# Two roots cut in two slots, the cheap scores ahead of a subtraction, and rows brought to all partitions by DMA instead of by TensorE

## The reference

```
# branch A: gated DeltaNet, 8 heads, prompt in chunks
q, k = l2_normalize(silu(conv(q))) * 128**-0.5, l2_normalize(silu(conv(k)))
beta = sigmoid(b);  g = -exp(a_log) * softplus(a + dt_bias)
G = cumsum(g)                              # per head and chunk
decay = where(i >= j, exp(G_i - G_j), 0)
L = where(i > j, (k*beta) @ k.T * decay, 0)
sol = triangular_solve(I + L, [v*beta, k*beta*exp(G)])
s, o = scan over the chunks with exp(G), decay, sol
y_a = rms_norm(o) * gdn_norm * silu(z)
# branch B: latent attention over the pages of a cache
for page in page_table:
    kn = rms_norm(c @ w_uk);  v = c @ w_uv
    s = (qn . kn + qr . kr) * scale;  partial softmax, merged at the end
# x + (g_a * (y_a @ w_ya) + g_b * (y_b @ w_yb)) @ w_o, then x + relu(..)**2 @ w_down
```

## Time and profile before

| | us |
|---|---|
| median of 3 runs | 1426.72 |
| lowest, highest run | 1419.31, 1428.12 |
| the profiled execution, own time | 1426.71 |
| its span in the profile | 1424.9 |
| what lies around the span | 1.8 |

### The profile page before, as it was taken

How to read it: one execution, slowest core, us unless ns; L and a number is a source line. 1 busy time by engine, 2 the same in 40 slices (tenths; PEclk the granted TensorE clock), 3 DMA queues, 4 the chain that set the end, 5 groups by cost and what they waited for, 6 DMA issues and landing times.

```text
span 1424.9 us, 30022 instructions
## 1 busy us (share of the span) xinstructions
PE 1385.5 (97%) x9428; PEld 1170.5 (82%) x9428; DVE 1013.0 (71%) x3674; ACT 859.0 (60%) x2780; POOL 296.0 (21%) x339
## 2 busy tenths in 40 slices
PE   8999999999999999999999999899999999999998
PEld 7877887877777777878778787678778999999998
DVE  5867667787877787777878777768666667777543
ACT  5536678686666866666865667566784453444332
POOL 3012222223332222322222312222241000000000
PEclk9999999999999999999999999999999999999999
DMA  9442326643457443365443463334644565555551
GB/s 284 119 118 57 92 53 146 161 104 73 95 116 162 105 98 76 87 154 125 93 108 85 107 141 83 74 80 104 178 89 157 167 237 177 178 178 177 177 180 59
DMA packets 282890, 180.05 MB, mean 126 GB/s; under 512 B 183072, under 2 KB 229696, under 8 KB 282728
## 3 DMA queue, kind: packets, MB, share of 16 engines
q1 hardware_dynamic: 282418, 177.86, 48.9%
q10 hardware_dynamic: 318, 0.33, 0.1%
HBM read 134.32 MB, written 6.77 MB: 99 GB/s over the span
## 4 chain that ended last, share of the span: by engine, by line
PE 78%; DVE 9%; ACT 8%; issue 3%; SPq 2%; DMA 1%; POOL 0%; DVEq 0%; ACTq 0%
PE ps L2058 13%; PE ps L2060 12%; PE ps L2059 12%; PE ps L2462 6%; PE ps L2463 6%; PE ps L2464 6%; ACT ksq L894 2%; PE ps L2133 2%; DVE prod L1284 2%; PE ps L2410 2%; PE ps L2411 2%; PE ps L2080 2%; PE ps L2134 2%; ACT cTr L881 2%; PE ps L2135 2%
## 5 line engine op out<-in xcount | busy, mean ns | idle before, releaser
L2058 PE MATMUL ps<-ukh,cTh 128*128 128x512 f32 x1024 | 418.7, 409 | 21.4 <-DVE sparts L1284 21.1
L894 ACT ACTIVATE ksq<-ps 128x128 f32<-128x128 f32 x1024 | 268.2, 277 | 243.3 <-PE ps L2060 242.9
L2060 PE MATMUL ps<-ukh,cTl 128*128 128x512 f32 x1024 | 402.2, 393 | 0.0
L2059 PE MATMUL ps<-ukl,cTh 128*128 128x512 f32 x1024 | 402.2, 393 | 0.0
L2058 PEld LDWEIGHTS ps<-ukh,cTh 128*128 128x128 f32 x1024 | 194.3, 190 | 77.7 <-issue 37.4
L1284 DVE CUSTOM_DVE_ANT_0 prod<-ps,qb 128x128 f32<-128x128 f32 x1024 | 234.9, 286 | 6.1 <-ACT ksq L894 5.1
L2060 PEld LDWEIGHTS ps<-ukh,cTl 128*128 128x128 f32 x1024 | 193.8, 189 | 43.0
L2059 PEld LDWEIGHTS ps<-ukl,cTh 128*128 128x128 f32 x1024 | 194.3, 190 | 34.2
L746 POOL TENSOR_TENSOR rk<-kss,mhalf 128x8 f32<-128x8 f32 x128 | 219.5, 1715 | 10.7
L894 ACT ACTIVATION_READ_ACCUMULATOR ksq<-ps 128x1 f32 x1024 | 212.9, 208 | 0.0
L881 ACT ACTIVATE cTr<-turned 128x1024 uint16<-128x1024 uint16 x126 | 174.6, 1386 | 3.6 <-DMA turned<-planes 3.6
(11 more groups left out here) (504 smaller groups left out, 2700.8 us busy)
## 6 DMA issues: line engine op xcount, KB each, us to landing
clat<-cache_mla SPq DMA_DIRECT2D x128, 256.0 KB, 2.6
wraw<-w_in SPq DMA_DIRECT2D x16, 1024.0 KB, 5.2
wraw<-w_up SPq DMA_DIRECT2D x16, 1024.0 KB, 5.4
wraw<-w_down SPq DMA_DIRECT2D x16, 1024.0 KB, 5.0
braw<-w_in SPq DMA_DIRECT2D x24, 512.0 KB, 4.1
crope<-cache_mla SPq DMA_DIRECT2D x128, 32.0 KB, 2.4
qb<-scratch SPq DMA_DIRECT2D x16, 256.0 KB, 3.7
sst<-state_gdn SPq DMA_DIRECT2D x32, 128.0 KB, 3.5
```

The lines of the kernel that those rows point to most:

```text
L894: i = nc.scalar.activation(ksq[m % 3], ps[:, k % 3, P * h:P * h + P], ACT.Square, accum_out=kss[:, n // 4 % 2, n % 4, h0 + h:h0 + h + 1]). ...
L2058: mm(out, cTh[:, n % 2, c], ukh[:, c, cols], start=c == 0, stop=False)
L2059: mm(out, cTh[:, n % 2, c], ukl[:, c, cols], start=False, stop=False)
L2060: i = mm(out, cTl[:, n % 2, c], ukh[:, c, cols], start=False, stop=c == 3)
```

## The change

- VectorE, page loop: `scored` of the group before now stands ahead of `split_lo(n + 1)`, with the same waits.
- `newton` is cut in two. `newton_start` does the reciprocal, at steps 16 and 44. The rest stands in the slot behind step 16, which was empty (`ROOT`), and at step 45. Steps 17 and 46, where TensorE takes the results, stay where they were.
- The four `spread_row` of a pair for decay sums and beta are gone, with VectorE's copies out of PSUM for the decay sums (L1515) and the split of `rw`. In their place, SP writes the 2 x 8 rows of `rw` to a tensor in HBM once (slot 34), waits until both writes have landed, and reads for each pair the two rows of decay sums into `eg` and a row of beta each into `br0` and `br1`, with a broadcast to all 128 partitions. This reading is at slot 34 for pair 0 and at step 44 of the pair before for the others. `br1` lies in SBUF where `rwh` lay, `br0` where `rwl` lay. VectorE reads beta from SBUF now.

```
-STEPS = list(range(14)) + [None, 14, 15, 16, None] + list(range(17, 47))
+ROOT = 47
+STEPS = list(range(14)) + [None, 14, 15, 16, ROOT] + list(range(17, 47))
...
+            def decay_rows_in(b):
+                if b >= 1:
+                    sp.wait_ge(S("a_read"), a_count(f"out3_{b - 1}"))
+                    sp.wait_ge(S("beta_read"), 2 * b)
+                sp.dma_start(eg[:], decay_rows[H + 2 * b:H + 2 * b + 2, :].rearrange("(o h) t -> o h t", o=1).to_broadcast([P, 2, T])).then_inc(S("eg_landed"), 16)
+                for hh in range(2):
+                    sp.dma_start(beta[hh][:], decay_rows[2 * b + hh:2 * b + hh + 1, :].to_broadcast([P, T])).then_inc(S("beta_landed"), 16)
...
                 if k == 44 and b + 1 < HP:
                     pair_rows_in(b + 1)
+                    decay_rows_in(b + 1)
...
                 if i == B_START - 1:
                     pair_weights(2)
+                    sp.wait_ge(S("g_ready"), 1)
+                    sp.wait_ge(S("decay_act"), 4)
+                    for r in range(2):
+                        sp.dma_start(decay_rows[H * r:H * r + H, :], rw[32 * r:32 * r + H, :]).then_inc(S("decay_rows_landed"), 16)
+                    sp.wait_ge(S("a_read"), a_count("bg"))
+                    sp.wait_ge(S("decay_rows_landed"), 32)
+                    decay_rows_in(0)
...
+            def newton_start(rows_, count):
+                v.wait_ge(S("row_sqrt"), count)
+                y = lr[0:rows_, 1]
+                V.reciprocal(y, y).then_inc(S("row_inverse"), 1)
+
             def newton(rows_, count, scale, sem):
-                v.wait_ge(S("row_sqrt"), count)
+                v.wait_ge(S("row_inverse"), count)
                 x, y, t_ = lr[0:rows_, 0], lr[0:rows_, 1], lt3[0:rows_]
-                link(V.reciprocal(y, y))
...
                 if k in (12, 13):
                     hh = k - 12
-                    V.tensor_copy(eg[:, hh, :], bank(f"gr{hh}")[:, 0:T]).then_inc(S("a_read"), 1)
-                    v.wait_ge(S("a_read"), a_count(f"gr{hh}_{b}"))
+                    v.wait_ge(S("eg_landed"), 16 * (b + 1))
...
                 if k == 16:
+                    newton_start(P, 2 * b + 1)
+                if k == ROOT:
                     newton(P, 2 * b + 1, consts[:, C_RSQ], "row_rstd")
                 if k in (15, 16):
...
-                    p_ = bank(f"br{hh}")
+                    v.wait_ge(S("beta_landed"), 32 * (b + 1))
+                    p_ = beta[hh]
...
                 if k == 44:
+                    newton_start(64, 2 * b + 2)
+                if k == 45:
                     newton(64, 2 * b + 2, 1.0, "row_rstd")
...
                 beside(2 * n)
-                if n + 1 < NT:
-                    split_lo(n + 1)
                 if n == 1:
                     scored(0, 0)
                 if n:
                     scored(n - 1, 1)
+                if n + 1 < NT:
+                    split_lo(n + 1)
...
-                if k in (12, 13):
-                    pe.wait_ge(S("rw_split"), 1)
-                    spread_row(f"gr{k - 12}_{b}", P, 32 + 2 * b + k - 12, rwh[:], rwl[:])
...
-                if k in (15, 16):
-                    spread_row(f"br{k - 15}_{b}", P, 2 * b + k - 15, rwh[:], rwl[:])
```

More of the change, by code:

```diff
@@ L136 @@
 F_END = F_ATT + H + 3
-STEPS = list(range(14)) + [None, 14, 15, 16, None] + list(range(17, 47))
+ROOT = 47
+STEPS = list(range(14)) + [None, 14, 15, 16, ROOT] + list(range(17, 47))
 B_START, B_SLOTS = F_END + 6, len(STEPS)
-PAIR_A = ([f"p{j}" for j in range(6)] + ["gr0", "gr1", "l2r", "br0", "br1", "lb0", "lb1", "lb2", "lb3", "qk", "kk", "qks", "kqs", "kqsT", "x1", "t1"])
+PAIR_A = ([f"p{j}" for j in range(6)] + ["l2r", "lb0", "lb1", "lb2", "lb3", "qk", "kk", "qks", "kqs", "kqsT", "x1", "t1"])
 for _s in range(2, LEVELS):
@@ L301, in build @@
         assert e <= C_NEG.stop * 4
-        rwh, e = place("rwh", [P, T], F32R, C_NEG.start * 4)
+        br1, e = place("br1", [P, T], F32, C_NEG.start * 4)
         assert e <= C_NEG.stop * 4
@@ L352, in build @@
         bwl, o = place("bwl", [P, KC, P], F32R, o)
-        rwl, _ = place("rwl", [P, T], F32R, o)
+        br0, _ = place("br0", [P, T], F32, o)
         rw, o = place("rw", [P, T], F32, o)
@@ L417, in build @@
         ps = ctx.enter_context(nc.psum_tensor("ps", [P, 8, 512], F32))
+        beta = [br0, br1]
+        decay_rows = nc.dram_tensor("decay_rows", (2 * H, T), F32, kind="Internal").ap()
         scratch = nc.dram_tensor("scratch", (NS, D), F32, kind="Internal").ap()
@@ L1440, in decay_steps @@
                     V.tensor_copy(bg[:].rearrange("p n c -> p (n c)"), a_bank("bg")[:, 0:128]).then_inc(S("a_read"), 1)
-                    v.wait_ge(S("decay_act"), 4)
-                    split(rw[:], rwh[:], rwl[:], "rw_split")
             def conv(b, j):
@@ L1530, in pair_dve @@
                     v.wait_ge(S("decay_exp"), 3 * b + 1)
-                    p_ = bank(f"br{hh}")
+                    v.wait_ge(S("beta_landed"), 32 * (b + 1))
+                    p_ = beta[hh]
                     us = slice(2 * hh, 2 * hh + 2)
                     V.tensor_tensor(lT[:, us, :].rearrange("p u n -> p (u n)"), dt_[:, us, :].rearrange("p u n -> p (u n)"), p_[:, 0:TP], ALU.mult)
-                    V.tensor_copy(small(7)[:, :, hh], p_[:, TP:T]).then_inc(S("a_read"), 1)
+                    V.tensor_copy(small(7)[:, :, hh], p_[:, TP:T]).then_inc(S("beta_read"), 1)
                 if k == 17:
-                    v.wait_ge(S("a_read"), a_count(f"br1_{b}"))
+                    v.wait_ge(S("beta_read"), 2 * b + 2)
                     link(V.tensor_tensor(lT[:], lT[:], level_mask(C_STRICT), ALU.mult))
```

## The result

The changed kernel takes 1436.03 us (median of 10 runs, 1432.01 to 1438.68), the kernel before 1426.52 us beside it (1419.31 to 1429.33). The ratio is 1.0069 with a 95% interval of 1.0053 to 1.0084: some 9.8 us slower, within 1%, where 3.6 us faster was forecast. The predicted range ended at 1436.0.

A forecast was written before the change was run, and what follows sets the result against it. TensorE, busy for 97% of the span, was taken as the bound. Gains of 1.9, 2.5, 3.5 and 0.4 less losses of 2.2 and 2.5 made 3.6 us gained, from 1426.7 to 1423.0 us; range 1410 to 1436.

The forecast's parts named there:

- the first root: Steps 16 and 17: cutting the root lets scores past; even pairs lose, odd pairs gain; 2.5 us gained, from -5 to +12.
- SP ahead of pair 0: Slot 34: writes, wait and reads put the page off by 3.7 us; 2.5 us lost, from 0 to 5.
- SP at the end of a pair: Step 44: three more DMAs ahead of `turn` and pages; 2.2 us lost in pair 1, 0 in pair 2.
- the wait at 619: Sign at the end of pair 1: TensorE's wait there would be longer by 1.2 to 3 us.
- The second root: Steps 44 to 46: the cut gains 0.9 us in pair 0, 2.6 in pair 2; sum 3.5, between 0 and 7.
- Scores ahead of the low half: VectorE's page loop: scores (0.84 us) fill holes while it waits for ScalarE; 0.4 us gained, from -1 to 2.
- The products: Steps 12 to 16: 16 products off TensorE at 0.24 us each; bounds 0 and 3.84, half taken, 1.9 us gained.
- B: Rival: broadcasts hold SP's one queue and pages land 3 us later, deciding from 0.7 us an issue; 1433 us, chance 0.22.
- C: Rival: TensorE's waits for scores become as long waits for roots at steps 17 and 46; 1426 to 1428 us, chance 0.16.

The follow-up runs named there:

- cut_only: The kernel before with both roots cut in two as in the change, nothing else: 1428.99 us, ratio 1.0022.
- after_rows_later: The whole change, but each pair's reads of rows (pair 0's with the wait for the landing) at the pair's own step 6: 1422.35 us, ratio 0.9978.
- trip_only: `after_rows_later`, but SP waits in slot 34 for the landing of its two writes; the reads stay at step 6: 1423.61 us, ratio 0.9998.
- later_cut_second: `after_rows_later` with the first root whole and only the second cut: 1422.51 us, ratio 0.9974.
- cut_gap: `after_rows_later` with the pair's empty slot moved from ahead of step 14 to between `ROOT` and step 17: 1415.52 us, ratio 0.9940.
- later_uncut: `after_rows_later` with both roots whole: 1420.00 us, ratio 0.9954.
- order_only: The kernel before with only the scores moved ahead of the low half in VectorE's page loop: 1421.91 us, ratio 0.9974.
- slot_more: `cut_gap` with the empty slot ahead of step 14 kept as well, so 50 slots a pair instead of 49: 1410.64 us, ratio 0.9894.
- products_more: `slot_more` with the rows by 16 products on TensorE as before, instead of the DMAs: 1413.11 us, ratio 0.9907.
- short_reads: `after_rows_later` plus three short reads (4 KB in all) at the end of pairs 0 to 2, where the change reads: 1422.46 us, ratio 0.9983.

## Why the prediction was wrong

The steps that failed most are the two terms for SP's queue: together they had 4.7 us lost, and taking the reads from those places gave 13.0. Next to them, the term for the first root had 2.5 gained where some 4 were lost. Each in turn:

- **SP ahead of pair 0: forecast 2.5 lost, measured 6.7.** The term had the mechanism (page late, TensorE waits for the scores), but took the trip from the query row's 1.85 us and left the page's landing at the usual 2.5 to 3.5 us behind its issue. The first write is issued at 239.45, the second 0.55 later at 240.00, and the reads follow at 243.50: 3.5 us for the trip. And 528 KB ahead of it delay the landing by 1.8 us, which the working had nowhere in this term. Its upper bound of 5, "slow clock included", was too low for a 4.44 us wait with a stretch at 0.66 behind it. The Trainium skill, "DMA: Bandwidth & Descriptors" (the anatomy of one DMA), with its 2.0 us of fixed cost (a fit for DMAs issued from GpSimd), would have been nearer by 0.15 us and still short by 1.5.
- **SP at the end of a pair: forecast 2.2 lost in pair 1 and 0 in pair 2; measured about 2.2 and 2.3 to 3.8.** In pair 1 the table gives -0.64 against -2.91 with those reads away, the forecast's 2.2. The match is in part luck: the page's issue is late by 1.2 us, its landing by another 2.1, where the term had 1.4 and 0.8, and slack takes the rest. The sign that the wait at 619 would be longer did not come (2.00 us at 627.00), since the new order alone gains 3.05 us there. The 0 for pair 2 was wrong: that pages were ahead and "only `turn` is late" is what happened, but VectorE's planes wait for `turn` with no slack, 2.43 us already before at 811.27. I had looked at SP's order and not at who waits for the transpose.
- **The first root: forecast 2.5 gained, `cut_only` shows some 4 lost.** The signs by pair were right: even pairs lose, odd ones don't. So was VectorE's order behind the reciprocal, which the changed kernel shows in pair 0 as it was worked out (multiplication, scores and low half, then the rest):

```profile
318.20 1.80 DVE L1490 RECIPROCAL lr<-lr 128x264 f32<-128x264 f32 x1 [0.80 <-ACT lr L1005]
...
321.16 0.69 DVE L1291 TENSOR_TENSOR cTl<-cTr,cTh 128x512 fp32r<-128x512 f32 x1
321.77 0.43 DVE L1495 TENSOR_TENSOR lt<-lr 128x264 f32<-128x264 f32 x1
```

  What failed is the clock in these terms. In `cut_only`, TensorE at pair 0's root and two 10-us stretches, of pair 0 and pair 1 (after the length: PE, PEld, DVE, ACT, POOL busy, granted clock, DMA share, GB/s):

```profile
316.92 0.39 PE L2116 MATMUL ps<-lrh,idr 128*128 128x264 f32 x1 [2.67 <-DVE lrl L1173]
```

```profile
317.00:327.00 10.00, 10.00 (x49) 8.57 (x50) 8.54 (x39) 5.88 (x22) 4.12 (x6) 0.83 0.21 41
...
507.00:517.00 10.00, 8.56 (x34) 6.80 (x34) 8.68 (x35) 6.19 (x24) 5.84 (x6) 0.83 0.34 66
```

  In pair 0 the group behind the root loses 1.2 us against before (forecast 0.7) and the two behind it 1.5 more at a clock of 0.83, where I had charged none. In pair 2 it is 2.2 and 1.0, for a forecast of 1.0 in all. In pair 1 the group at step 16 comes 2.2 us earlier, as forecast, and the wait at step 17 takes 1.9 of it back; the slow stretch at 507, whose 1.5 us I had booked as saved, is there as before. Only pair 3 (+1.9 forecast, 1.64 measured) held. What the clock is worth there shows in `after_rows_later` and `trip_only`, which have the same program at these roots: with a stretch at 0.83 pairs 0 and 2 lose 2.34 and 3.34 us, at 1.00 it is 0.74 and 1.60, near the forecast's 0.7 and 1.0.
- **The second root: forecast 3.5 gained.** Pair 0's 0.9 came (1.04 in `cut_only`). Pair 2's 2.6 did not: 0.65 lost. Pair 1, booked at nothing, gains 2.06, with the slow stretch behind it gone. All four columns make 2.1 in `cut_only`. With the reads at step 6 and the order exchanged, the second cut loses 2 to 3 us over all (`later_cut_second`), and in `cut_gap` it makes no difference. The order alone already gains 3.05 us at pair 1's end, which may be part of it; why the versions differ was not settled.
- **Scores ahead of the low half: forecast 0.4, measured 3.7**, past the upper bound of 2. I had counted one 0.84 for each wait. VectorE's 110 us of standing for `cTh`, most of which falls to this order, was a row of the profile that I did not read.
- **The products: forecast 1.9 within 0 to 3.84.** `later_uncut` against `order_only` gives 1.9 us by the medians and 2.9 by the ratios, `slot_more` against `products_more` 2.5 and 1.9, the latter not clear of the noise. The size is right, the reason only in part. Each group behind two of them comes 0.5 us earlier, as the 0.24 said, but in the trace of `later_uncut` the next root's wait takes all of it back in pairs 0, 1 and 3 and 0.7 of 1.8 in pair 2. What is left over is gained at the ends of the pairs (0.6 to 1.0 us each), where no product stood, and was not explained.
- **The rivals.** The time is nearest to B (1433), and its place is right: the broadcasts hold SP's queue. Its price is not. It was to decide from 0.7 us an issue; issues follow each other every 0.45 us, and `short_reads` shows that the bytes, not the issues, make most of the loss. C names what happened at the roots: the waits changed their names.

The parts by themselves (3.7 gained by the order, 3.1 lost by the cut, 14.1 by the rows, all by the ratios) add up to 13.5 lost, the change loses 9.8. They share slack, so they need not add.

## What to carry to other kernels

Price a new DMA by what stands behind it in its queue: count its bytes into the landing of the next page or transpose, find who waits for that one, and put it where nobody waits, here two slots later or at the pair's own step 6. A long operation cut in two paid here only once the second part's taker was moved off too: with its result due in the next slot the cut lost 2 to 3 us, with an empty slot between the cut version was 7 us ahead of the whole one with the same slots, though only 2 to 4.5 us, hardly clear of the noise, ahead of the best whole one. Try the slot by itself as well; one more of them gained the uncut roots 6 us. And read the waits of the engine that feeds the bottleneck: an exchange of two lines there gained 3.7 us.

## What the runs showed of the hardware

- A DMA transpose takes longer to land with plain traffic issued ahead of it: 3.49 us from its issue to the next planes without the reads, 4.37 with three short ones ahead, 6.47 with 528 KB more.
- A write of 8 rows to HBM and the instruction that waits for it lie 3.5 us apart here, behind 512 KB of weights in the same queue, where the trip of the earlier trace rows took 1.85. Whether the weights are the reason was not tried.
- The length of a wait alone does not tell what clock follows. Three versions with the same program around pair 2's root waited 3.50, 3.51 and 3.52 us there, and the granted clock averaged 0.66, 0.83 and 1.00 over 10 us. The change has the first (at 707.97); the waits and stretches of `after_rows_later` and of `trip_only`:

```profile
699.05 0.39 PE L2133 MATMUL ps<-lrh,idr 128*128 128x264 f32 x1 [3.51 <-DVE lrl L1192]
...
698.00:708.00 10.00, 8.95 (x40) 0.83 0.20 40
```

```profile
698.67 0.39 PE L2133 MATMUL ps<-lrh,idr 128*128 128x264 f32 x1 [3.52 <-DVE lrl L1192]
...
698.00:708.00 10.00, 9.32 (x55) 1.00 0.34 66
```

  Likewise 1.92 us at pair 0's root were followed by 0.83 in the change, and 1.91 in `trip_only` by 1.00; and before, had 0.83 after 2.44 where 2.48 had none. Pair 2's root lost 4.94, 3.34 and 1.60 us in these three (the table), so such a stretch cost 1.6 to 1.7 us at 0.83 and twice that at 0.66, and a forecast can only give it a chance.
